# Sparse attention heads: mask and relative bias summed in device memory, loaded as one tile

## The chip, the cores and the metric

The kernel runs on one core of one Trainium2 chip. The metric is the device time in microseconds (us); a kernel is given by the median of its runs. One further execution is recorded by the hardware profiler, and all rows come from it. The engines are TensorE (PE; PEld is its weight load), VectorE (DVE), ScalarE (ACT), GpSimd (POOL) and SyncE (SP), which only issues transfers. SPq in a row is SP's instruction queue.

## What is computed

One encoder layer over 16 meta tokens and 1,024 tokens of width 1,024: a norm, one wide input projection, eight dense attention heads (branch A), eight sparse attention heads (branch B), gates, an output projection, and a mixture of experts. The change touches the scores of the sparse heads only:

```python
score = jnp.where(adm[None], score, NEG_INF)
_, idx = lax.top_k(score, k_sel)                      # 256 keys for each query
s = jnp.einsum('bqhd,bqkhd->bhqk', qb, ks) * scale_b
bias = rel_bias[t5_bucket(idx - pq[None, :, None])]   # by distance, one value a head
s = s.astype(jnp.float32) + jnp.transpose(bias, (0, 3, 1, 2)).astype(jnp.float32)
s = jnp.where(valid[:, None], s, NEG_INF)
p = jax.nn.softmax(s, axis=-1)
```

The kernel gathers nothing. It computes the scores of all keys and adds a mask of 0 or -1e30, so that the keys that were not selected vanish in the softmax.

## The kernel before

**Tiling.** Queries are cut into eight blocks of 128 rows. Block i may see the first WID[i] = 16 + 128 (i + 1) keys: 144, 272, 400, 528, 656, 784, 912 and 1,040. OFF holds the running sums of these widths; all eight side by side are OFF[8] = 4,736 columns. The mask is one tile of 128 x 4,736 in bf16 (`mask`). It depends on the query and the key, not on the head. The bias depends on the distance and the head, not on the block: `rel_d` in device memory holds for each head 128 copies of a row of 1,168 values, and `skewed[h]` reads it with a row pitch one shorter than the row, which gives the 128 x 1,040 table of block 7; block i uses the same table from column 128 (7 - i) on.

**Three stages matter.** (1) Projections, to about 548 us: PE runs `jobs`, ACT writes each result to one of four `stage` tiles, SP stores it (L391) and loads the next 1 MB weight piece (`piece_in`, L352); beside it DVE searches the top-k thresholds and writes `mask`. POOL forms the low-order parts of the weight pieces (L732). (2) Dense heads, 548 to about 701 us. (3) Sparse heads, to about 861 us. Stages 2 and 3 are one block of code with one pipeline: a table `turns`, built in Python, lists half heads s (s = 2 x head for blocks 0 to 3, s = 2 x head + 1 for blocks 4, 5, 7 and 6, `ORDER`), and in each half head one turn for each tile of 128 keys (5 or 9). `qk_after` says behind which turn a block's scores are computed ahead of use.

**Work of a block (`qk`, `row_max`, `exp`).** PE writes the scores of block g into PSUM. In a sparse head these are three passes of WID columns: identity times mask (L1144), query times leading part of the keys (L1147), query times rest of the keys (L1149). DVE adds the bias table `tb` to them, writes `sbias` and takes the row maximum in one instruction (L1284), and negates it (L1288). ACT takes the exponential into px, pxa or pxb, with the row's sum (L1233). In a dense head there is no bias; DVE only takes the maximum (L1291) and ACT reads PSUM.

**Work of a turn.** PE transposes up to four 128 x 128 tiles (L1191) into one of three PSUM banks; ACT copies the leading part (pH, L1245); DVE subtracts it (pL, L1310); three turns later PE multiplies both with the values (L1207, L1208). At a half head's end ACT copies the sum (oT, L1253), PE transposes it back (L1193), DVE adds two halves (otmp, L1317), POOL scales (otok, L1330).

**What sets the order.** Each engine runs its list in the written order. ACT's list has the copies pH and the exponentials in one row, and DVE's has pL and the row maxima in one row. PE opens a half head only when its four exponentials are done.

**POOL** prepares the next heads' inputs: at odd s the values (L1344 to L1349) and the next queries (L1355, L1357; L1361, L1363 for sparse heads), at even s the next keys (L1374, L1376), and `scaled` at each s. Its 16 half heads of the dense stage are s = 0 to 15. **SP** loads in the sparse stage, for each head in turn, QR (L1098), KR (L1103), tb (L1109) and VR (L1113, L1115), each behind the wait that frees its tile, all double buffered. With head 1 of the sparse ones it also loads the first branch weights (`wbr`, L1005).

## Time and profile before

| | |
|---|---|
| median of 3 runs | 1481.53 us (1480.89 to 1482.75) |
| the profiled execution | 1482.05 us |
| its span in the profile | 1480.3 us |
| PE, DVE, ACT, POOL busy | 93%, 70%, 45%, 28% of the span |
| dense heads | about 548 to 701 us |
| sparse heads | about 701 to 861 us |

The page of the profile gives the busy time of each engine, the span in 40 slices, the groups of instructions, and the transfers. Beside it, the trace can be asked for stretches (busy time of each engine in a window), for instructions in order of time, for waits, and for transfers. "[0.51 <-PE ps L1149]" at the end of a row means that the engine stood idle for 0.51 us before it and that PE's instruction of line 1149 ended this. A busy time holds the latency of each instruction, so that a pipelined engine can be busy without being at its peak.

### The profile page before, as it was taken

Reading aid. Unit: us, or ns where it says so; the run is one execution under the profiler, and the core shown is the slowest. Engines: PE = TensorE matmul, PEld = TensorE weight load, DVE = VectorE, ACT = ScalarE, POOL = GpSimd, SP = SyncE. Lnnn points to the kernel's source line nnn. Section 1 sums busy time; section 2 is a strip of 40 time slices with the busy share of each in tenths; the row PEclk is TensorE's granted clock in tenths of the full one; section 3 lists DMA queues with packets and bytes.
Section 4 is the critical chain, followed back from the end, with each engine's and each line's share of the span. In section 5 each row is a group of like instructions: output and inputs, shape, how many; then the busy total and the mean of one; then the engine's idle time right before and its main releaser. Section 6 shows DMA issues by size and latency. Waiting matters only on the chain. (4 is left out here: it accounts for less than half of the span.)

```text
span 1480.3 us, 21833 instructions
## 1 busy us (share of the span) xinstructions
PE 1383.0 (93%) x7358; PEld 1124.1 (76%) x7367; DVE 1029.0 (70%) x1959; ACT 665.5 (45%) x1179; POOL 416.9 (28%) x472
## 2 busy tenths in 40 slices
PE   5989999999999999999999979999959999999973
PEld 3779888888989758888788868899946777777741
DVE  4448999999980367777888863443287777777746
ACT  4347413322111146777777751022125666666622
POOL 1100335421112015545555303300021323323313
PEclk9999999999999999999999989999959999999996
DMA  6131321123232100303244044322178999999918
GB/s 210 30 124 57 126 77 50 48 88 104 73 97 93 51 0 2 80 1 108 55 98 102 23 147 147 110 100 82 48 292 345 364 355 348 364 376 369 349 54 329
DMA packets 89744, 217.42 MB, mean 147 GB/s; under 512 B 25825, under 2 KB 50945, under 8 KB 77369
## 3 DMA queue, kind: packets, MB, share of 16 engines
q1 hardware_dynamic: 79392, 194.65, 37.7%
q0 software_dynamic: 9216, 16.80, 3.0%
q10 hardware_dynamic: 1048, 4.82, 0.8%
q8 instruction: 53, 0.87, 0.3%
q14 instruction: 35, 0.28, 0.1%
HBM read 193.06 MB, written 44.73 MB: 161 GB/s over the span
## 5 line engine op out<-in xcount | busy, mean ns | idle before, releaser
L421 PE MATMUL ps<-hHi,g_lead 128*128 128x512 f32 (+2 forms) x480 | 184.8, 385 | 7.9 <-DVE g_rest L818 6.7
L315 DVE TENSOR_SCALAR_CACHE_REDUCE mask<-score,cand 128x272 bf16<-128x272 f32 (+6 forms) x224 | 185.5, 892 | 4.6 <-DVE cand L334 4.4
L2290 DVE TENSOR_TENSOR w_rest<-wgu,w_lead 128x1024 fp32r<-128x1024 f32 x128 | 156.2, 1223 | 46.6 <-ACT w_lead L2235 45.5
L422 PE MATMUL ps<-hLo,g_lead 128*128 128x512 f32 (+2 forms) x480 | 184.1, 384 | 0.0
L423 PE MATMUL ps<-hHi,g_rest 128*128 128x512 f32 (+2 forms) x480 | 183.0, 381 | 0.0
L1310 DVE TENSOR_TENSOR pL<-ps,pH 128x512 fp32r<-128x512 f32 (+3 forms) x224 | 124.6, 572 | 51.9 <-ACT pH L1245 49.3
L2235 ACT CAST w_lead<-wgu 128x1024 fp32r<-128x1024 f32 x124 | 130.8, 1055 | 48.6 <-PE ps L2178 48.6
L732 POOL TENSOR_TENSOR g_rest<-g_raw,g_lead 128x2048 fp32r<-128x2048 f32 x12 | 55.7, 4642 | 299.6 <-ACT g_lead L588 299.6
L1245 ACT CAST pH<-ps 128x512 fp32r<-128x512 f32 (+3 forms) x224 | 106.2, 493 | 59.3 <-PE ps L1191 59.1
L2176 PE MATMUL ps<-w_lead,x_lead 128*128 128x512 f32 x256 | 114.5, 447 | 4.0 <-DVE x_rest L2297 4.0
L2198 PE MATMUL ps<-wd,hmT 128*128 128x512 f32 x256 | 115.3, 593 | 1.6 <-DVE hmT L2313 1.0
L421 PEld LDWEIGHTS ps<-hHi,g_lead 128*128 128x128 f32 x480 | 91.0, 190 | 24.9 <-issue 7.0
L423 PEld LDWEIGHTS ps<-hHi,g_rest 128*128 128x128 f32 x480 | 91.2, 190 | 16.7
L422 PEld LDWEIGHTS ps<-hLo,g_lead 128*128 128x128 f32 x480 | 91.0, 189 | 15.0
L2178 PE MATMUL ps<-w_lead,x_rest 128*128 128x512 f32 x256 | 102.3, 400 | 0.0
L2177 PE MATMUL ps<-w_rest,x_lead 128*128 128x512 f32 x256 | 101.5, 396 | 0.0
L1207 PE MATMUL ps<-pH,VS 128*128 128x512 f32 (+3 forms) x224 | 94.6, 423 | 0.0
L2140 POOL DMA_INDIRECT ys_d<-ye,dk x32 | 32.3, 1010 | 216.0 <-DVE ye L2325 216.0
L2198 PEld LDWEIGHTS ps<-wd,hmT 128*128 128x128 f32 x256 | 46.2, 190 | 47.8 <-issue 47.8
L1208 PE MATMUL ps<-pL,VS 128*128 128x512 f32 (+3 forms) x224 | 79.1, 353 | 0.0
L619 ACT ACTIVATE stage<-ps 128x512 f32<-128x512 f32 x32 | 19.2, 599 | 112.0 <-PE ps L423 112.0
L2176 PEld LDWEIGHTS ps<-w_lead,x_lead 128*128 128x128 f32 x256 | 49.4, 193 | 21.0 <-issue 7.2
(363 smaller groups left out, 3421.1 us busy)
## 6 DMA issues: line engine op xcount, KB each, us to landing
wgu<-in_w_exp_gate SPq DMA_DIRECT2D x32, 1024.0 KB
wgu<-in_w_exp_up SPq DMA_DIRECT2D x32, 1024.0 KB
wd<-in_w_exp_down SPq DMA_DIRECT2D x32, 1024.0 KB, 12.0
g_raw<-in_w_in SPq DMA_DIRECT2D x16, 1024.0 KB, 5.6
gates_d<-stage SPq DMA_DIRECT2D x32, 256.0 KB, 2.0
gt<-gates_d SPq DMA_DIRECT2D x32, 256.0 KB, 3.2
rel_d<-rel_s ACTq DMA_DIRECT2D x1, 4672.0 KB
KR<-kb_d SPq DMA_DIRECT2D x16, 260.0 KB, 6.5
```

The source lines that it names most:

```text
L315: return dve.tensor_scalar(mask[:, OFF[i]:OFF[i + 1]], score[:, OFF[i]:OFF[i + 1]], thr, 0.0, op, ALU.add, accum_out=cnt[:, i:i + 1])
L421: pe.matmul(dst, x[0], y[0], start=(k == 0), stop=False)
L422: pe.matmul(dst, x[0], y[1], start=False, stop=False)
L423: return pe.matmul(dst, x[1], y[0], start=False, stop=(k == KT - 1))
L1245: act.copy(pH[n % RING][:, lo:512], bank_of(k)[:, lo:512]).then_inc(s_ld, 1)
L1310: dve.tensor_tensor(pL[n % RING][:, lo:512], bank_of(k)[:, lo:512], pH[n % RING][:, lo:512].bitcast(F32), ALU.subtract).then_inc(s_rs, 1)
L2176: pe.matmul(dst, xl[:, k, :], wl, start=(k == 0), stop=False)
L2177: pe.matmul(dst, xl[:, k, :], wr, start=False, stop=False)
L2178: mm = pe.matmul(dst, xr[:, k, :], wl, start=False, stop=(k == KT - 1))
L2198: mm = pe.matmul(ps[:, 5 + half, :], hmT[u % 2][:, k, :], wd[u][:, k, 512 * half:512 * (half + 1)], start=(k == 0), stop=(k == 1))
L2235: act.copy(w_lead[part][:, :, :, :], wgu[u][:, :, 2 * part:2 * part + 2, :]).then_inc(S["m_wl"], 1)
L2290: dve.tensor_tensor(w_rest[u][:, :, 2 * part:2 * part + 2, :], wgu[u][:, :, 2 * part:2 * part + 2, :], w_lead[part][:, :, :, :].bitcast(F3 ...
```

## The change

1. **Projections.** Beside jobs 4 to 35 SP issues two transfers each, 64 in all, from `rel_d` to a new array `bias_d` in device memory. It holds for each head the bias as 128 rows of 4,736 values in the mask's layout, 2.42 MB a head. The block's end waits for them.
2. **Dense heads.** POOL first writes `mask` to a new array `mask_d`, from bf16 to f32. Then, at the end of its half heads s = 3, 5, ... 17, it issues one accumulating transfer, `bias_d[h] += mask_d`, in device memory. Each waits for the one before (`s_jn`). As built it goes in 512 pieces of 1,184 values (4,736 bytes) each. `s_md` is waited for once, at s = 3.
3. **Sparse heads, loads.** In place of tb SP loads the sum into one tile `tbm`, 128 x 4,736 in f32, in four pieces a head, for blocks 0 and 1, 2 and 3, 4 and 5, and 6 and 7. There is one such tile; a piece is loaded when DVE has used the same piece for the head before (`s_mx`). The loads of queries, keys and values are spread between the pieces and keep their own waits. VR0 moves to where tb0 and VR0 lay.
4. **Sparse heads, compute.** The pass of L1144 is gone: two passes in place of three. DVE's instruction reads `tbm` instead of `tb`. It waits for the piece at every second block, not once a head.

```diff
@@ SP, projections
                     sp.dma_start(dst, src).then_inc(s_gds[n % 4], 16)
+                    if EARLY <= n < EARLY + 4 * H:
+                        if n == EARLY:
+                            sp.wait_ge(s_reld, 16)
+                        h, pair = divmod(n - EARLY, 4)
+                        for i in (2 * pair, 2 * pair + 1):
+                            c = P * (NB - 1 - i)
+                            sp.dma_start(bias_d[h, :, OFF[i]:OFF[i + 1]], skewed[h][:, c:c + WID[i]]
+                                         ).then_inc(s_bias, 16)
...
-                sp.wait_ge(s_reld, 16)
+                sp.wait_ge(s_bias, 16 * H * NB)
@@ SP, sparse heads (queries_in, keys_in and values_in hold the loads and waits of before)
+                def bias_in(h, pair):
+
+                    if h:
+                        sp.wait_ge(s_mx, 8 * (h - 1) + 2 * pair + 2)
+                    c = slice(OFF[2 * pair], OFF[2 * pair + 2])
+                    sp.dma_start(tbm[:, c], bias_d[h, :, c]).then_inc(s_tbs[pair], 16)
+
+                for h in range(2):
+                    queries_in(h)
+                    keys_in(h)
+                    values_in(h)
+                sp.wait_ge(s_hr, 2 * (H - 1))
+                for piece in range(2):
+                    load_branch_weights(sp, piece, s_wb)
+                for h in range(H):
+                    sp.wait_ge(s_jn, 16 * (h + 1))
+                    bias_in(h, 0)
+                    if 1 <= h < H - 1:
+                        values_in(h + 1)
+                    bias_in(h, 1)
+                    if h + 2 < H:
+                        queries_in(h + 2)
+                    bias_in(h, 2)
+                    if h + 2 < H:
+                        keys_in(h + 2)
+                    bias_in(h, 3)
@@ PE, qk of a sparse block
-                        for lo, hi in parts:
-                            pe.matmul(flat[:, o + lo:o + hi], identb[:, :], mask[:, OFF[i] + lo:OFF[i] + hi],
-                                      start=True, stop=False)
-                        for lo, hi in parts:
-                            pe.matmul(flat[:, o + lo:o + hi], q, kh[:, lo:hi], start=False, stop=False)
+                            pe.matmul(flat[:, o + lo:o + hi], q, kh[:, lo:hi], start=True, stop=False)
@@ DVE, row_max of a sparse block
                         if g % 8 == 0:
-                            dve.wait_ge(s_tb[h % 2], 16 * (h // 2 + 1))
                             dve.wait_ge(s_vr, 2 * H)
-                        c = P * (NB - 1 - i)
-                        dve.tensor_tensor_reduce(sbias[g % 2][:, 0:w], flat[:, o:o + w], tb[h % 2][:, c:c + w],
+                        if g % 2 == 0:
+                            dve.wait_ge(s_tbs[i // 2], 16 * (h + 1))
+                        dve.tensor_tensor_reduce(sbias[g % 2][:, 0:w], flat[:, o:o + w], tbm[:, OFF[i]:OFF[i + 1]],
@@ POOL, heads
+                def joined(h):
+
+                    if h:
+                        pool.wait_ge(s_jn, 16 * h)
+                    pool.dma_start(bias_d[h], mask_d[:, :], max_dma_last_dim=4736,
+                                   accum_op=ALU.add).then_inc(s_jn, 16)
+
+                pool.dma_start(mask_d[:, :], mask[:, :]).then_inc(s_md, 16)
...
                     if s >= 1:
                         scaled(s - 1)
+                    if s == 3:
+                        pool.wait_ge(s_md, 16)
+                    if s % 2 == 1 and 3 <= s < HH + 3:
+                        joined(s // 2 - 1)
```

The built programs show it at three places. PE, in the first sparse head, around the scores of block 6 (912 columns in two parts; con is the identity, QS the queries), before:

```order
L1191 MATMUL ps<-con,px_4845 128x128
L1144 MATMUL ps<-mask,identb 128x456 x2
L1147 MATMUL ps<-KH_138,QS_4872 128x456 x2
L1149 MATMUL ps<-KL_140,QS_4872 128x456 x2
L1207 MATMUL ps<-pH_4854,VS_4840 128x512
```

The same place now:

```order
L1221 MATMUL ps<-con,px_4910 128x128
L1177 MATMUL ps<-KH_138,QS_4937 128x456 x2
L1179 MATMUL ps<-KL_140,QS_4937 128x456 x2
L1237 MATMUL ps<-pH_4919,VS_4905 128x512
L1238 MATMUL ps<-pL_4923,VS_4905 128x512
```

The two instructions of the mask pass are gone, and nothing else moved. POOL, in the dense heads, from the queries of one head (q_lead, q_rest) to the keys (KH, KL) of the same head, before:

```order
L1355 CAST q_lead_135<-QTa 96x1024
L1357 TENSOR_TENSOR q_rest_137<-QTa,q_lead_135 96x1024
L1330 TENSOR_TENSOR otok_71<-otmp_4864,rec 128x4x64
L1374 CAST KH_139<-KTa 64x1040
L1376 TENSOR_TENSOR KL_141<-KTa,KH_139 64x1040
```

The same place now:

```order
L1385 CAST q_lead_135<-QTa 96x1024
L1387 TENSOR_TENSOR q_rest_137<-QTa,q_lead_135 96x1024
L1360 TENSOR_TENSOR otok_71<-otmp_4929,rec 128x4x64
L1413 DMA bias_d<-mask_d 512x1184
L1404 CAST KH_139<-KTa 64x1040
L1406 TENSOR_TENSOR KL_141<-KTa,KH_139 64x1040
```

The accumulating transfer, with its wait for the one before, stands ahead of the keys. SP, at the change from dense to sparse heads, before (the values of sparse head 1, the branch weights, then the loads of head 2):

```order
L1109 DMA tb_4877<-rel_d 128x1040
L1113 DMA VR_4879<-vb_d 128x8x64
L1115 DMA VR_4879<-vb_d 16x64
L1005 DMA wbr_4880<-in_w_branch_a 128x4x256
L1005 DMA wbr_4880<-in_w_branch_b 128x4x256
L1005 DMA wbr_4881<-in_w_branch_a 128x4x256
L1005 DMA wbr_4881<-in_w_branch_b 128x4x256
L1098 DMA QR_4870<-qb_d 64x1024 x2
L1103 DMA KR_4868<-kb_d 64x1040 x2
```

The same place now:

```order
L1123 DMA VR_4942<-vb_d 128x8x64
L1125 DMA VR_4942<-vb_d 16x64
L1019 DMA wbr_4944<-in_w_branch_a 128x4x256
L1019 DMA wbr_4944<-in_w_branch_b 128x4x256
L1019 DMA wbr_4945<-in_w_branch_a 128x4x256
L1019 DMA wbr_4945<-in_w_branch_b 128x4x256
L1132 DMA tbm<-bias_d 128x416
L1132 DMA tbm<-bias_d 128x928
L1109 DMA QR_4935<-qb_d 64x1024 x2
L1132 DMA tbm<-bias_d 128x1440
L1116 DMA KR_4933<-kb_d 64x1040 x2
L1132 DMA tbm<-bias_d 128x1952
```

The whole joined tile of the first sparse head is loaded here, behind the branch weights; before, its table had been loaded some 90 us earlier.

## Rows read from the trace of the kernel before

**Rows 1.** The page: busy us (share of the span) xinstructions of each engine.

```profile
PE 1383.0 (93%) x7358; PEld 1124.1 (76%) x7367; DVE 1029.0 (70%) x1959; ACT 665.5 (45%) x1179; POOL 416.9 (28%) x472
```

**Rows 2.** Stretches; columns: window, length, PE, PEld, DVE, ACT, POOL busy, PEclk, DMA share, GB/s.

```profile
200.00:240.00 40.00, 40.00 (x195) 35.46 (x194) 38.59 (x101) 11.48 (x33) 16.38 (x38) 1.00 0.14 47
572.00:610.00 38.00, 37.43 (x263) 31.91 (x262) 28.32 (x52) 27.49 (x65) 19.90 (x20) 1.00 0.33 78
720.00:740.00 20.00, 18.97 (x130) 15.96 (x130) 16.34 (x45) 14.61 (x36) 10.68 (x11) 1.00 0.41 97
740.00:760.00 20.00, 19.65 (x136) 16.69 (x136) 15.55 (x43) 14.66 (x34) 11.09 (x13) 1.00 0.45 111
```

**Rows 3.** PE in order of time around block 6: start us, us, instruction.

```profile
774.11 0.55 PE L1144 MATMUL ps<-mask,identb 128*128 128x456 bf16 x2
...
775.32 0.39 PE L1207 MATMUL ps<-pH,VS 128*128 128x512 f32 x1
```

**Rows 4.** PE, ACT and DVE in order of time, one sparse head.

```profile
758.64 0.66 PE L1191 MATMUL ps<-con,pxb 128*128 128x128 f32 x4
...
759.95 0.69 DVE L1310 TENSOR_TENSOR pL<-ps,pH 128x512 fp32r<-128x512 f32 x1 [0.81 <-ACT pH L1245]
...
761.09 0.42 ACT L1233 ACTIVATE px<-sbias,negm 128x144 f32<-128x144 f32 x1 [0.17 <-DVE negm L1288]
...
766.31 0.74 ACT L1233 ACTIVATE px<-sbias,negm 128x528 f32<-128x528 f32 x1 [0.33 <-DVE negm L1288]
...
769.78 0.84 ACT L1233 ACTIVATE pxb<-sbias,negm 128x656 f32<-128x656 f32 x1 [1.22 <-DVE negm L1288]
...
771.38 0.69 DVE L1310 TENSOR_TENSOR pL<-ps,pH 128x512 fp32r<-128x512 f32 x1
...
775.52 1.11 DVE L1284 CUSTOM_DVE_ANT_0 sbias<-ps,tb 128x912 f32<-128x912 f32 x1
...
776.86 1.06 ACT L1233 ACTIVATE pxb<-sbias,negm 128x912 f32<-128x912 f32 x1
...
778.06 0.66 PE L1191 MATMUL ps<-con,pxb 128*128 128x128 f32 x4 [0.76 <-ACT pxb L1233]
```

**Rows 5.** Waits from 701 to 862 us: who <- whom: us, times, longest.

```profile
PE ps L1191 <- ACT pxb L1233: 3.0, 4, 0.8
DVE sbias L1284 <- PE ps L1149: 2.1, 4, 0.5
```

**Rows 6.** POOL in order of time, two dense heads.

```profile
603.37 0.61 POOL L1330 TENSOR_TENSOR otok<-otmp,rec 128x256 f32<-128x256 f32 x1 [8.73 <-DVE otmp L1317]
...
622.82 0.61 POOL L1330 TENSOR_TENSOR otok<-otmp,rec 128x256 f32<-128x256 f32 x1 [8.74 <-DVE otmp L1317]
...
642.49 0.61 POOL L1330 TENSOR_TENSOR otok<-otmp,rec 128x256 f32<-128x256 f32 x1 [8.74 <-DVE otmp L1317]
```

**Rows 7.** Transfers from 90 to 130 us, by queue: packets, MB, share of 16 engines.

```profile
q10 hardware_dynamic: 1032, 4.78, 30.9%
```

**Rows 8.** One line of the code, POOL's gathers of 128 rows: duration ns min/median/max.

```profile
L2128 POOL DMA_INDIRECT xs<-xn_d,tk x28: 1017/1414/1419, 1102.2 to 1394.7; - x28
```

**Rows 9.** SP's loads in order of time, at the change to the sparse heads.

```profile
686.11 0.42 SPq L1005 DMA_DIRECT2D wbr<-in_w_branch_a x1
...
689.24 2.50 SPq L1098 DMA_DIRECT2D QR<-qb_d  x2
```

**Rows 10.** Stretches at the change to the sparse heads; columns as in Rows 2.

```profile
688.00:692.00 4.00, 4.00 (x29) 3.44 (x27) 3.30 (x7) 2.55 (x6) 3.68 (x4) 1.00 0.99 287
692.00:696.00 4.00, 4.00 (x29) 3.66 (x28) 3.01 (x7) 2.83 (x6) 0.42 (x1) 1.00 1.11 337
```

**Rows 11.** One line of the code, DVE's bias and maximum: duration ns min/median/max.

```profile
L1284 DVE CUSTOM_DVE_ANT_0 sbias<-ps,tb x64: 295/738/1232, 702.8 to 852.4; 128x144 f32<-128x144 f32 x8, 128x272 f32<-128x272 f32 x8, 128x400 f32<-128x400 f32 x8, 128x528 f32<-128x528 f32 x8
```

**Rows 12.** The page, costliest groups: busy, mean ns, idle before and its releaser.

```profile
L732 POOL TENSOR_TENSOR g_rest<-g_raw,g_lead 128x2048 fp32r<-128x2048 f32 x12 | 55.7, 4642 | 299.6 <-ACT g_lead L588 299.6
```

**Rows 13.** The page, transfers: KB each, us from issue to landing.

```profile
g_raw<-in_w_in SPq DMA_DIRECT2D x16, 1024.0 KB, 5.6
```

More of the change, by code:

```diff
@@ L128, in hybrid_layer @@
         rel_s = dram("rel_s", (H, REL), F32)
+        bias_d = dram("bias_d", (H, P, OFF[NB]), F32)
+        mask_d = dram("mask_d", (P, OFF[NB]), F32)
         qb_d = dram("qb_d", (4, P, T), F32)
@@ L305, in hybrid_layer @@
             sem, ["s_ij", "s_ie", "s_il", "s_wp", "s_wi", "s_lg", "s_re", "s_sc"])
-        s_gj, s_ge, s_tk, s_fl, s_uw = map(sem, ["s_gj", "s_ge", "s_tk", "s_fl", "s_uw"])
+        skewed = [bass.AP(tensor=rel_d.tensor, offset=h * P * REL + P - 1, ap=[[REL - 1, P], [1, L]])
+                  for h in range(H)]
+        s_gj, s_ge, s_tk, s_fl, s_uw, s_bias = map(sem, ["s_gj", "s_ge", "s_tk", "s_fl", "s_uw", "s_bias"])
         s_gds = [sem(f"s_gd{k}") for k in range(4)]
@@ L997, in hybrid_layer @@
         sbias = [at(f"sbias{k}", [P, L], F32, R_V + 4160 * k) for k in range(2)]
-        tb = [at(f"tb{k}", [P, L], F32, (R_Q + 8192, R_V + 8320)[k]) for k in range(2)]
-        VR = [at(f"VR{k}", [P, 9, HD], F32, (R_Q + 12352, R_V + 12480)[k]) for k in range(2)]
+        VR = [at(f"VR{k}", [P, 9, HD], F32, (R_Q + 8192, R_V + 12480)[k]) for k in range(2)]
+        tbm = at("tbm", [P, OFF[NB]], F32, R_Q + 12288)
+        assert 12288 + 4 * OFF[NB] <= 33280
         wbr = [at(f"wbr{k}", [P, 2, 4, 256], F32, R_K + 16640 + 8192 * k) for k in range(2)]
@@ L1006, in load_branch_weights @@
                              [:, :, 256 * piece:256 * (piece + 1)]).then_inc(done, 16)
-        s_qr, s_kr, s_vd, s_tb = ([sem(f"s_{nm}{k}") for k in range(2)] for nm in ("qr", "kr", "vd", "tb"))
+        s_qr, s_kr, s_vd = ([sem(f"s_{nm}{k}") for k in range(2)] for nm in ("qr", "kr", "vd"))
+        s_tbs = [sem(f"s_tb{pair}") for pair in range(4)]
+        s_md, s_jn = sem("s_md"), sem("s_jn")
         s_wb = sem("s_wb")
-        skewed = [bass.AP(tensor=rel_d.tensor, offset=h * P * REL + P - 1, ap=[[REL - 1, P], [1, L]])
-                  for h in range(H)]
         HH = 2 * H
@@ L1092, in _, with queries_in, keys_in, values_in @@
             def _(sp):
-                for h in range(H):
-                    j, u, k, hh = h // 2, h % 2, h % 2, H + h
-                    sp.wait_ge(s_hr, 6 if h < 2 else 2 * (hh - 2) - 1)
+                def queries_in(h):
+                    sp.wait_ge(s_hr, 6 if h < 2 else 2 * (H + h - 2) - 1)
                     for dup in range(2):
-                        sp.dma_start(QR[k][64 * dup:64 * (dup + 1), :], qb_d[j, 64 * u:64 * (u + 1), :]
-                                     ).then_inc(s_qr[k], 16)
+                        sp.dma_start(QR[h % 2][64 * dup:64 * (dup + 1), :],
+                                     qb_d[h // 2, 64 * (h % 2):64 * (h % 2 + 1), :]).then_inc(s_qr[h % 2], 16)
+                def keys_in(h):
                     if h >= 2:
-                        sp.wait_ge(s_hr, 2 * (hh - 2))
+                        sp.wait_ge(s_hr, 2 * (H + h - 2))
                     for dup in range(2):
-                        sp.dma_start(KR[k][64 * dup:64 * (dup + 1), :], kb_d[j, 64 * u:64 * (u + 1), :]
-                                     ).then_inc(s_kr[k], 16)
-                    if h == 1:
-                        sp.wait_ge(s_vr, 2 * H)
-                    if h >= 2:
-                        sp.wait_ge(s_mx, 8 * (h - 1))
-                    sp.dma_start(tb[k][:, :], skewed[h]).then_inc(s_tb[k], 16)
-                    if h >= 2:
-                        sp.wait_ge(s_vr, 2 * (hh - 1))
-                    c = slice(HD * h, HD * (h + 1))
+                        sp.dma_start(KR[h % 2][64 * dup:64 * (dup + 1), :],
+                                     kb_d[h // 2, 64 * (h % 2):64 * (h % 2 + 1), :]).then_inc(s_kr[h % 2], 16)
+                def values_in(h):
+                    k, c = h % 2, slice(HD * h, HD * (h + 1))
+                    if h:
+                        sp.wait_ge(s_vr, 2 * H if h == 1 else 2 * (H + h - 1))
                     sp.dma_start(VR[k][:, 0:8, :], vb_d[0:T, c].rearrange("(t p) c -> p t c", p=P)
@@ L1115, in _ @@
                     sp.dma_start(VR[k][0:META, 8, :], vb_d[T:L, c]).then_inc(s_vd[k], 16)
-                    if h == 1:
-                        sp.wait_ge(s_hr, 2 * (H - 1))
-                        for piece in range(2):
-                            load_branch_weights(sp, piece, s_wb)
+                def bias_in(h, pair):
[22 more added lines that the diff above has]
+                    bias_in(h, 3)
             @blk.tensor
```

1 line of the change is left out of this document (added).

## The prediction

> **What bounds the kernel now.** I read the page first. PE is busy 93% of the span [rows 1], and taken alone that would make every dropped PE pass a gain. The share is a mean over stages, so I went to the stretches of those that the change touches: the projections from 200 to 240 us, the dense heads, and the sparse heads. PE is busy 40.0 of 40, 37.4 of 38, and 19.0 to 19.65 of 20 us [rows 2]. The sparse heads seem as much bound by PE as the projections. But a busy PE there holds latencies and transposes, and a block of work has three engines in it. So I read one sparse head, 19.42 us long, in order of time [rows 4] and asked at each step who came last.
>
> It begins with PE's transposes at 758.64. ACT copies them, and DVE's pL at 759.95 has waited 0.81 us for ACT. Then DVE takes a row maximum, negates it, and ACT's exponential at 761.09 has waited 0.17 us for it. The next exponential at 766.31 waited 0.33 us for DVE, and that at 769.78 waited 1.22 us. From 771.38 DVE runs the maxima of blocks 5, 7 and 6 and the pL between them; the maximum of block 6 starts at 775.52 with no wait for PE. ACT's exponential at 776.86 follows it, and PE's transposes at 778.06 stood idle for 0.76 us for ACT before the next head began. What closes the loop is therefore ACT and DVE in turn, with PE in it once a head, for the first transposes. The reverse wait, DVE for PE's scores, is 2.1 us in all eight heads, four times, 0.5 at most; PE's wait for the last exponential of a head is 3.0 us [rows 5].
>
> **The mask pass.** Around block 6 the three passes take from 774.11 to 775.32, 1.21 us [rows 3]: 0.40 us a pass for 912 columns, 0.44 ns a column. A head has 4,736 columns, so 2.1 us a head, and for eight heads 16.8 us. That is the most that it can bring, if PE were the bound.
>
> What it brings in the loop above is less. The scores' end decides only where DVE waits for it: 2.1 us in all [rows 5]. Where ACT waits for PE's transposes, the passes ahead of these make them later, but DVE is then still at its own list (block 5 to 7: it goes from 771.38 to the last maximum with pL and maxima alone), so what ACT gains it waits for at DVE. Since scores come earlier, a part of the 2.1 us stays in the loop at ACT and DVE. I take 1.0 us, between 0 and 2.1. PE's idle time grows by nearly the 16.8 us instead.
>
> DVE's instruction reads another tile of the same shape and type, with nothing else changed: 0. Its wait at each second block finds the piece loaded long before, except in the first head (below). Behind the wait stand pL and the maxima of the same list. I take 0, at most 1 us over 32 waits.
>
> **The projections.** SP issues 64 transfers more among those of the weight pieces. They read and write 19.4 MB each way over some 30 jobs. PE is at 40.0 of 40 us in this stage, with the transfer engines at a share of 0.14 and 47 GB/s [rows 2]. A weight piece lands 5.6 us after its issue [rows 13]; POOL, which works on it, idles 299.6 us in 12 waits for ACT in this stage [rows 12], so a piece may land some us later without anyone noticing. Cover: PE's own matmuls, and the pieces' buffers. I take 0. Without the cover a piece late by its own 5.6 us would cost PE that much once or twice; I keep up to 3 us for it in the range.
>
> **The accumulating transfers.** Eight of them, issued by POOL, about one per head of the dense stage. The trace shows no such transfer, so I bound its time T. The nearest packets in size are those of the broadcast to `rel_d`: 1,032 packets took 30.9% of 16 engines' time in 40 us [rows 7], 197.8 engine-us, 0.192 us for each 4.6 KB. The new transfer has 512 pieces of 4.7 KB, 32 per engine. One pass is 6.1 us, if reading both operands costs no more than a copy; two passes are 12.3 us, if each operand is one; three are 18.4 us, if the sum is written in a pass of its own. To these comes POOL's own work for the pieces: its gathers of 128 rows hold it 1.4 us [rows 8], so 512 pieces are between 1.4 and 5.6 us. T lies between 7.5 and 24.0 us; I take the middle, near two passes and 3.5 us, 15.8.
>
> The rows say what T would have to be to hurt. POOL waits before each transfer for the one before. POOL's `otok` of one place in the dense head comes at 603.37, 622.82 and 642.49 [rows 6], so the transfers are issued 19.45 to 19.67 us apart, and below that T costs nothing. Above it POOL is late by T - 19.5 at each of seven waits. It idles 8.7 us a head before that place [rows 6]; since the lateness adds up, this slack is used once: the cost is 7 x (T - 19.5) - 8.7 us. It is nothing to T = 20.7, +3 us at 21.2, +12.3 at 22.5 and +22.8 at 24.0. At my value it is 0. Behind POOL's wait stand the keys of the next head (KH, KL) and the scaling, and behind the keys PE's scores.
>
> The Trainium skill, page "Collectives: The Full Stack", section "The bandwidth ceiling: the fold count and why AG ≠ RS ≠ AR", says that an add in the transfer engines costs no time for the adding, but needs two source reads and so goes at half a copy's rate. By it T is at most 12.3 + 5.6 = 17.9 us, as an estimate, against at most 11.7 us at a copy's price; either is under a head's length, and the third pass, with which alone the change could turn slower, would not exist. No row here shows an adding transfer, so I keep the third pass in the bounds.
>
> The cast of the mask into device memory is one more transfer of POOL at the start, with the first values following behind it on POOL. It is of the size of one pass, and runs beside PE's first dense scores: 0, since it only holds POOL for the issue, 1.4 to 5.6 us against the 8.7 us that POOL idles per head [rows 6].
>
> **The first loads of the sparse heads.** SP issues the branch weights from 686.11 and the loads of the next head from 689.24 [rows 9]. From 688 to 696 us the transfer engines are full, a share of 0.99 to 1.11, at 287 to 337 GB/s [rows 10]. The change puts the first head's sum there, 2.4 MB, where 0.5 MB of the next table lay: 1.9 MB more, at 337 GB/s 5.6 us more of full engines, and beside it one accumulating transfer, issued in the same microseconds. DVE needs the first piece (blocks 0 and 1, 0.2 MB) at 702.8 [rows 11]; that is 13 us behind the issue. The later pieces are needed some us after that. Bounds: 0, and +5 us if the whole of the extra traffic ends in front of DVE. I take +0.5, since the first piece stands ahead of the queries and is small. At later heads a piece is loaded nearly a head ahead, with the share at 0.41 to 0.45 [rows 2]: 0.
>
> The Trainium skill, page "DMA: Bandwidth & Descriptors", section "Issuing engines are not separate DMA queues", says that transfers of all issuing engines run on the same 16 and interleave. By that rule the pieces from SP and the accumulating transfer from POOL share the full stretch, which speaks for a cost here. The trace agrees that the stretch has no room, but shows no accumulating transfer.
>
> **The sum.** Mask pass -1.0, waits and projections 0, accumulating transfers 0, first loads +0.5: -0.5 us. On the profiled execution of 1482.05 us that is 1481.5. This execution stands 0.5 us above the median of the runs shown, 1481.53, so I forecast 1481.0 us: no change that can be told, since 0.2% (about 3 us) is what a measurement of this kernel can tell from none.
>
> **Rivals.**
>
> *PE is the bound after all.* For it: 19.65 us busy in 20 [rows 2], and PE's single wait of a head, 0.76 us [rows 4], is short; with the passes gone ACT's and DVE's waits for PE shrink too. Against it: at the head's end PE waits for ACT, and ACT's exponentials wait 0.3 to 1.2 us for DVE. Fully, 1481.5 - 16.8 = 1464.7 us; by half, about 1473. Chance 0.15.
>
> *An accumulating transfer outlasts a dense head.* This is the case on the slower side. Place: POOL's wait for the transfer before, at the end of each second half head from 610 us on, ahead of the next keys. Price: 7 x (T - 19.5) - 8.7 us. It decides from T = 20.7 us. With T = 22.5, 1481.5 + 12.3 = 1493.8 us; at the upper bound of T, about 1504. For it: three passes and a slow issue are within the bounds, and in the dense heads these transfers share the engines with others, at a share of 0.33 [rows 2]. Against it: it needs nearly the upper ends of both terms. Chance 0.21.
>
> *The first loads come late.* DVE stands at its first maxima for the pieces: up to +5 us, 1486. Chance 0.06.
>
> *It doesn't do what it says* would be that the pass is dropped but comes back as time elsewhere on PE; the order shows only the two instructions gone, so I give it no chance of its own.
>
> **How the numbers follow.** Forecast 0.58, PE-bound 0.15, accumulating 0.21, late loads 0.06. The forecast's own range is 1478.5 to 1484.5: the mask pass 0 to -2.1, up to 3 us for projections and the extra waits. The range reaches below to the half gain, 1474 with a little of it spared, and above to 1492, where the accumulating rival is at T = 22.2. Left out are the full gain (0.08) and the larger part of the accumulating rival (0.11). Faster by over 0.2%: the PE-bound rival and 0.02 of the forecast, 0.17. Slower: the accumulating rival less 0.01 where T is just at the limit, and the late loads: 0.26. Within: 0.57.
>
> **What the profile after would show.** Right: in the sparse heads PE's busy time falls from 19.0 to 19.65 to about 17 of 20 us, while the distance between the first transposes of two heads stays at 19.0 to 19.4 us; PE's waits for ACT and DVE grow by some 15 us over the stage; DVE's waits for PE's scores vanish. POOL's wait for a transfer in the dense heads stays within its idle time, with the landing of the accumulating transfer at 8 to 19 us and the heads at 19.5 to 19.7 us. The sparse heads begin at about 701 us, with a wait of DVE for a piece below 1 us. Wrong: the head's length falls by up to 2.1 us (then PE was the bound, and the loop that I read was not tight); POOL waits for transfers over 8.7 us and PE for the keys (then T was too low); PE waits in the projections for weight pieces (then the 64 transfers weren't hidden).

## The result and the profile after

| | before | changed |
|---|---|---|
| median | 1481.63 us (4 runs) | 1494.75 us (4 runs, 1492.86 to 1496.42) |
| ratio | | 1.0085, 95% interval 1.0073 to 1.0097 |
| the profiled execution, its span | 1482.05, 1480.3 us | 1492.86, 1491.1 us |
| DVE's first L1284 / L1314 to its last | 702.8 to 852.4 us | 708.0 to 864.6 us |

The change costs 13 us, 0.85%. The forecast was 1481.0 us with a range to 1492.0, so the prediction is wrong. The page's engine line, beside [rows 1]:

```profile
PE 1371.6 (92%) x7254; PEld 1113.6 (75%) x7255; DVE 1021.2 (68%) x1959; ACT 664.5 (45%) x1179; POOL 426.6 (29%) x481
```

PE is busy 11.4 us less and the kernel is slower. (Dropping the pass alone takes 16.8 us off PE's busy time, in experiment 8; behind the waits below the matmuls take longer.) The stretches, with the columns of [rows 2]; the last one is a sparse head that nothing disturbs:

```profile
600.00:660.00 60.00, 59.08 (x413) 50.44 (x413) 45.95 (x82) 43.61 (x105) 33.98 (x33) 1.00 0.81 167
660.00:700.00 40.00, 39.26 (x274) 33.23 (x273) 30.17 (x55) 28.69 (x68) 22.67 (x22) 1.00 0.79 180
700.00:720.00 20.00, 14.17 (x82) 12.33 (x82) 9.68 (x32) 8.37 (x21) 11.26 (x11) 0.83 1.04 261
720.00:740.00 20.00, 16.99 (x110) 13.64 (x108) 15.36 (x41) 14.35 (x35) 11.32 (x11) 1.00 1.05 284
740.00:760.00 20.00, 13.90 (x88) 11.79 (x89) 13.29 (x37) 11.31 (x26) 7.23 (x9) 0.95 1.04 261
800.00:820.00 20.00, 17.42 (x117) 14.79 (x118) 15.98 (x44) 14.22 (x33) 11.35 (x11) 1.00 0.70 205
```

The dense heads go on at their pace. From 700 to 760 us the transfer engines are full (share 1.04 to 1.05, against 0.41 to 0.45 in [rows 2]), and PE, DVE and ACT have all lost busy time. DVE in order of time names what it waits for, at blocks 0 of head 0 and 2 of heads 1 and 2:

```profile
708.00 0.31 DVE L1314 CUSTOM_DVE_ANT_0 sbias<-ps,tbm 128x144 f32<-128x144 f32 x1 [6.16 <-DMA tbm<-bias_d]
...
731.87 0.57 DVE L1314 CUSTOM_DVE_ANT_0 sbias<-ps,tbm 128x400 f32<-128x400 f32 x1 [1.34 <-DMA tbm<-bias_d]
...
756.34 0.57 DVE L1314 CUSTOM_DVE_ANT_0 sbias<-ps,tbm 128x400 f32<-128x400 f32 x1 [5.11 <-DMA tbm<-bias_d]
```

These are 12.6 us in three waits, and there is no further one. The waits of the kernel before [rows 5] have none of this kind. The stretch from DVE's first L1314 to its last is 156.6 us, where L1284 took 149.6 before; with the first wait of 6.16 us, which lies ahead of it, 162.8. That is 13.2 us more, where the pass should have given something back.

Why the first piece is late: SP's list at the change to the sparse heads, and how long the three pieces issued from 685 to 693 us took to land (min/median/max):

```profile
684.69 0.42 SPq L1019 DMA_DIRECT2D wbr<-in_w_branch_a  x1
...
687.31 2.95 SPq L1132 DMA_DIRECT2D tbm<-bias_d  x2
...
735.09 7.64 SPq L1132 DMA_DIRECT2D tbm<-bias_d  x1
742.77 4.13 SPq L1109 DMA_DIRECT2D QR<-qb_d  x2
746.95 1.86 SPq L1132 DMA_DIRECT2D tbm<-bias_d  x1
```

```profile
DMA to landing us min/median/max: 19.2/20.5/21.6
```

The first piece is issued at 687.3 us, behind 2 MB of branch weights, and 0.2 MB takes about 20 us. An accumulating transfer is issued at 687.9 us. In the later rows SP itself is held: at 735.09, as soon as DVE is through with blocks 2 and 3 of head 1, the piece for these blocks of head 2 is issued; the issue alone lasts 7.64 us, the piece lands 21.1 us behind its start, and DVE still waits for it until 756.3. The queries and the next piece stand behind it on SP.

The accumulating transfers in the quiet dense heads and the one of 687.9 us, issue to landing; and the share of the engines that their queue (q0, GpSimd's) took from 560 to 702 us:

```profile
DMA to landing us min/median/max: 15.1/15.1/16.5
```

```profile
DMA to landing us min/median/max: 21.3/21.3/21.3
```

```profile
q0 software_dynamic: 2995, 13.81, 50.3%
```

50.3% of 142 us, times 16, over 2,995 packets is 0.381 us a packet, twice the 0.192 of the broadcast's [rows 7], and 512 of them are 12.2 us of all 16 engines. In this kernel POOL never waits for one; between two of them it idles for DVE, as before:

```profile
590.10 1.18 POOL L1413 DMA_DIRECT2D bias_d<-mask_d  x1
...
602.39 0.61 POOL L1360 TENSOR_TENSOR otok<-otmp,rec 128x256 f32<-128x256 f32 x1 [7.55 <-DVE otmp L1347]
...
609.54 1.04 POOL L1413 DMA_DIRECT2D bias_d<-mask_d  x1
```

### The profile page after: what moved, and what is told of

The parts are those of the page before. It is cut to its first block and busy times, and to the rows that moved or that the text cites. A ratio compares the mean times of both kernels' runs of the same rounds, so it can differ in the third digit from the quotient of the medians.

```text
span 1491.1 us, 21721 instructions
## 1 busy us (share of the span) xinstructions
PE 1371.6 (92%) x7254; PEld 1113.6 (75%) x7255; DVE 1021.2 (68%) x1959; ACT 664.5 (45%) x1179; POOL 426.6 (29%) x481
## 5 line engine op out<-in xcount | busy, mean ns | idle before, releaser
L632 ACT ACTIVATE stage<-ps 128x512 f32<-128x512 f32 x32 | 19.2, 599 | 112.1 <-PE ps L436 112.0
L1360 POOL TENSOR_TENSOR otok<-otmp,rec 128x256 f32<-128x256 f32 x32 | 19.6, 613 | 159.3 <-DVE otmp L1347 159.3
## 6 DMA issues: line engine op xcount, KB each, us to landing
wd<-in_w_exp_down SPq DMA_DIRECT2D x32, 1024.0 KB, 12.4
```

## The experiments

Ratios are against the kernel before on the same chip. *Theory A*: three of the eight accumulating transfers, 12 us of full engines each, fall into the stretch in which the sparse heads load, and with those loads they are more than the engines can move. *Theory B*: the loads alone are too much, since the bias of a head is 2.42 MB in place of 0.53.

**1. Without the accumulating transfers**

```diff
-                    if s % 2 == 1 and 3 <= s < HH + 3:
-                        joined(s // 2 - 1)
...
@@ SP
-                    sp.wait_ge(s_jn, 16 * (h + 1))
```

> The changed kernel without its eight accumulating transfers, and without SP's waits for them; the mask is left out of the result, the loads of the bias tile and the 64 transfers of the projections stay. Theory A (the last three accumulating transfers, 12 engine-us each, fill the engines in which the first three sparse heads load): DVE's waits for pieces fall from 12.6 us to 0 to 2, the time to 1481 to 1484. Theory B (the loads alone are too much: branch weights, doubled bias bytes, small packets): waits stay at 8 us or more, 1490 to 1495.

Measured: 1480.28 us, ratio 0.9988 (0.9978 to 0.9997), and no wait of DVE for a piece. Pieces issued from 685 to 693 us land in:

```profile
DMA to landing us min/median/max: 8.1/9.3/12.7
```

8 to 13 us in place of 19 to 22, though the first of them goes out at 690.0 us and not at 687.3. Theory B falls: branch weights, large pieces and all 64 transfers of the projections are still there. What the engines had to move from 684 to 765 us, by queue, before, here, and in the changed kernel:

```profile
q1 hardware_dynamic: 8203, 9.38, 45.4%
```

```profile
q1 hardware_dynamic: 11145, 17.56, 74.2%
```

```profile
q1 hardware_dynamic: 9309, 14.31, 56.8%
q0 software_dynamic: 1584, 7.27, 45.3%
```

By the first two, the bias as a 2.42 MB tile adds 28.8% of 81 us, 23 us of full engines, in four heads; this fits. Three accumulating transfers are 37 us more: 74.2% + 45.3% is 119.5%, some 16 us more than the stretch holds. The changed kernel's loads got only 56.8% in that time.

**2. The same transfers, earlier**

```diff
-        s_md, s_jn = sem("s_md"), sem("s_jn")
+        s_md, s_jn = sem("s_md"), [sem(f"s_jn{h}") for h in range(H)]
...
-                    if h:
-                        pool.wait_ge(s_jn, 16 * h)
...
-                    if s % 2 == 1 and 3 <= s < HH + 3:
-                        joined(s // 2 - 1)
+                    if 1 <= s <= H:
+                        joined(s - 1)
```

> The changed kernel with the accumulating transfers issued at each half head from the first on, with no wait between them (a semaphore for each), so that they are done by about 680 us if 12 to 13 us of full engines is their price. Theory A: the stretch from 686 to 760 us loses three of them; DVE's waits 0 to 3 us, 1481 to 1484. Theory B: as without them, waits of 8 us or more, 1490. A new cost would show as POOL held by the issue, or PE waiting for keys, in the dense heads.

Measured: 1479.14 us, ratio 0.9984 (0.9974 to 0.9994). All eight sums are made, none of them issued behind 644 us, and DVE waits for no piece. Landing of the pieces issued from 685 to 693 us, and DVE's L1314 from first to last:

```profile
DMA to landing us min/median/max: 9.1/9.8/12.4
```

```profile
L1314 DVE CUSTOM_DVE_ANT_0 sbias<-ps,tbm x64: 297/739/1231, 703.5 to 852.3; 128x144 f32<-128x144 f32 x8, 128x272 f32<-128x272 f32 x8, 128x400 f32<-128x400 f32 x8, 128x528 f32<-128x528 f32 x8
```

148.8 us, 0.8 less than before [rows 11]. The dense heads with the transfer engines full for 60 us, and two stretches of the sparse heads:

```profile
600.00:660.00 60.00, 59.12 (x412) 50.38 (x411) 45.01 (x80) 43.89 (x103) 35.41 (x35) 1.00 1.06 228
700.00:720.00 20.00, 17.52 (x118) 14.80 (x116) 16.28 (x48) 14.35 (x34) 10.28 (x10) 1.00 0.71 206
740.00:760.00 20.00, 17.65 (x121) 15.38 (x122) 15.75 (x44) 14.33 (x36) 11.07 (x12) 1.00 0.70 207
```

PE is busy 59.12 of 60 us with the transfer engines at 1.06. So the same work costs nothing that can be seen in the dense heads and 13 us at their end: the place decides. This kernel is some 15 us below the changed one, and its interval against the kernel before lies wholly below 1. The loads issued beside the transfers are slow here too (one of the values took 36.2 us to land), but no engine waited for them.

**3. Two of the eight in place of three.** Each one head earlier, with its wait:

```diff
-                    if s == 3:
+                    if s == 1:
...
-                    if s % 2 == 1 and 3 <= s < HH + 3:
-                        joined(s // 2 - 1)
+                    if s % 2 == 1 and s < HH + 1:
+                        joined(s // 2)
```

> The changed kernel with each accumulating transfer issued one head earlier (at half heads 1, 3, ... 15), with its waits. Two of eight, about 24 us of full engines, then fall behind 686 us in place of three, and the last one is issued at about 714 us. Theory A (the sum of what the engines have to move behind 686 us decides): 12 us of backlog go, DVE's waits fall from 12.6 us to 0 to 5, 1480 to 1486. Theory B (the burst at 686 to 692 decides, with the accumulating transfer of 688 us in it): about as the changed kernel, 8 us of waits or more, since that transfer is still there: 1489 to 1494.

Measured: 1488.34 us, ratio 1.0041 (1.0027 to 1.0056). DVE's waits:

```profile
708.72 0.31 DVE L1314 CUSTOM_DVE_ANT_0 sbias<-ps,tbm 128x144 f32<-128x144 f32 x1 [4.87 <-DMA tbm<-bias_d]
...
733.27 0.57 DVE L1314 CUSTOM_DVE_ANT_0 sbias<-ps,tbm 128x400 f32<-128x400 f32 x1 [2.96 <-DMA tbm<-bias_d]
```

7.8 us in place of 12.6, in heads 0 and 1. Neither expectation is met; B's lower ends (8 us, 1489) miss by little, A's upper ones (5 us, 1486) by more. The first wait, 4.87 us, is nearly that of the changed kernel, since at 689.9 us an accumulating transfer is still issued into the burst; the one in head 2 is gone with the transfer that fell there (that in head 1 is 2.96 in place of 1.34). I read this as two places with a price each, the burst at 686 us and the backlog behind it; how a single profile divides the waits among the heads is loose (experiment 7), so the sum of 7.8 is the firmer number.

**4. The burst without the weights.** The 2 MB of branch weights loaded ahead of head 6's pieces:

```diff
-                for piece in range(2):
-                    load_branch_weights(sp, piece, s_wb)
                 for h in range(H):
+                    if h == 6:
+                        for piece in range(2):
+                            load_branch_weights(sp, piece, s_wb)
```

> The changed kernel with the 2 MB of branch weights loaded before the pieces of sparse head 6, not before those of head 0. Theory A: the first wait of DVE, 6.2 us, shrinks to 0 to 3 since 2 MB (5 to 6 us of full engines) go, the waits in heads 1 and 2 (1.3 and 5.1 us) shrink as well, since the backlog starts lower: 1484 to 1489. Theory B: all waits go, 1481 to 1484. If the weights don't matter: 1494.

Measured: 1482.22 us, ratio 0.9999 (0.999 to 1.0009), with all three accumulating transfers within some 3 us of where they were (688.9, 711.2 and 731.8 us). Pieces issued from 685 to 693 us, and all of DVE's waits for pieces (us, times):

```profile
DMA to landing us min/median/max: 4.3/6.3/8.1
```

```profile
  DMA tbm<-bias_d: 1.2, 1
```

The first piece is issued at 685.8 us, 3.1 us ahead of the accumulating transfer (0.5 in the changed kernel), and lands in time; DVE then frees its part of the tile in time for the next head's. In numbers this is Theory B's forecast and a miss of Theory A's. Theory B stays out by experiments 1 and 2, where the loads and the weights are all there and nobody waits. What fails is Theory A as a rule of bytes alone: 6 us of traffic taken from in front of the first piece remove 11.4 us of waits, where 12 us taken from behind it (experiment 3) removed 4.8.

**5. The first head's pieces earlier.** First, the four pieces moved ahead of the weights and their wait (and dropped for head 0 in the loop behind, which the cut leaves out):

```diff
+                sp.wait_ge(s_jn, 16)
+                for pair in range(4):
+                    bias_in(0, pair)
                 sp.wait_ge(s_hr, 2 * (H - 1))
                 for piece in range(2):
                     load_branch_weights(sp, piece, s_wb)
```

> The changed kernel with the four pieces of sparse head 0 loaded as soon as their sum is there (about 605 us), in the dense heads. Theory A: 2.4 MB leave the full stretch, the first wait of 6.2 us goes; heads 1 and 2 lose at least half of their 6.4 us: 1481 to 1487. Rival (only the order of the queue counts, and the backlog of accumulating transfers stays): the first wait goes, the other two stay, 1488 to 1490.

Measured: 1497.15 us, ratio 1.0107 (1.009 to 1.0124). It missed: I had not read what stands ahead of that place in SP's list, the wait for the tile of head 1's values. SP's rows:

```profile
685.23 3.35 SPq L1132 DMA_DIRECT2D tbm<-bias_d  x4
...
691.72 12.97 SPq L1019 DMA_DIRECT2D wbr<-in_w_branch_b  x1
```

The pieces went out at 685.2 us, not at 605. Head 0 waited for none, but the weights and all behind them came later: the last weights' issue held SP for 12.97 us, and heads 1 and 2 waited 16.1 us in three waits. The edit as it was meant puts the pieces ahead of those values, behind `sp.wait_ge(s_hr, 2 * (H - 1) - 1)`, since the tile shares its place with the dense queries:

> The changed kernel with the four pieces of sparse head 0 ahead of the values of sparse head 1 in SP's list, behind the wait for the last dense queries, so that they are issued at about 667 us. In the kernel with the pieces merely ahead of the weights they stood behind the wait for those values and were issued at 685.2, as late as in the changed kernel. 2.4 MB leave the full stretch. If only the bytes ahead of the pieces count: no wait in head 0, less than 4 us in heads 1 and 2, 1481 to 1486. If the accumulating transfers alone decide: heads 1 and 2 still wait 6 us or more, 1487 to 1490.

Measured: 1482.71 us, ratio 1.0008 (0.9999 to 1.0018); waits for pieces:

```profile
  DMA tbm<-bias_d: 2.1, 1
```

The pieces went out at 668.2 us. Head 0 and head 1 wait for none, head 2 for 2.1 us: the first expectation is met. Three accumulating transfers are still issued behind 686 us, so they alone don't make the 12.6 us either.

**6. Small pieces.** Heads 1 to 7 load 32 columns a piece and use head 0's bias and mask in all other columns:

```diff
-                    c = slice(OFF[2 * pair], OFF[2 * pair + 2])
+                    c = slice(OFF[2 * pair], OFF[2 * pair] + 32 if h else OFF[2 * pair + 2])
```

> The changed kernel where the pieces of sparse heads 1 to 7 are 32 columns wide (128 bytes a row; the rest of the bias tile keeps head 0's values, so bias and mask of head 0 are used in all heads), head 0's pieces whole. The accumulating transfers and all else stay. Theory A (neither the sums nor the bias bytes alone, but both together): head 0 waits as before, about 6 us, heads 1 and 2 don't: 1486 to 1489. If the sums alone were too much for the loads of queries, keys and values: waits of 5 us or more in heads 1 and 2, or POOL late with the keys.

Measured: 1488.61 us, ratio 1.005 (1.0034 to 1.0067).

```profile
709.08 0.31 DVE L1314 CUSTOM_DVE_ANT_0 sbias<-ps,tbm 128x144 f32<-128x144 f32 x1 [5.22 <-DMA tbm<-bias_d]
...
732.67 0.57 DVE L1314 CUSTOM_DVE_ANT_0 sbias<-ps,tbm 128x400 f32<-128x400 f32 x1 [2.08 <-DMA tbm<-bias_d]
```

Head 0 waits as expected (5.22 us), head 2 no more; that head 1 still waits 2.08 us was not expected; its pieces stand in SP's queue behind head 0's large ones, but that this is the cause was not tried. So the bytes of the later heads' pieces have a part of about 5 of the 12.6 us, and none without the accumulating transfers (experiment 1).

**7. Early transfers with the first pieces ahead of the weights, and the changed kernel again**

> The changed kernel with the accumulating transfers at half heads 1 to 8, a semaphore for each, and head 0's pieces at about 667 us. With the accumulating transfers moved alone DVE waited for no piece, so the second edit should find nothing to gain: within 1 us of that kernel, 1478 to 1481. More than 2 us below it would mean that the burst at 686 us costs something that no wait shows.

Measured: 1479.48 us, ratio 0.9985 (0.9976 to 0.9995); no wait for a piece. The kernel as built is not the one that this expectation describes. It takes the first edit of experiment 5 and not the second: head 0's pieces stand ahead of the weights but behind the values of head 1, and SP issues them at 686.6 us, not at 667:

```profile
686.58 1.84 SPq L1132 DMA_DIRECT2D tbm<-bias_d  x4
```

So it shows this much: with the accumulating transfers early, the order that cost 16.1 us of waits in experiment 5 costs nothing, and pieces ahead of the weights gain nothing over experiment 2 (1479.14 us). Pieces at 667 us together with early accumulating transfers were not tried.

> The changed kernel again, for a profile and a ratio beside the others on one chip: 1492 to 1497, DVE waiting for pieces of heads 0 to 2 by 10 us or more. If the waits lie in other heads or their sum moves by over 5 us, single profiles of this collision can't be compared to a few us.

Measured: 1496.11 us, ratio 1.0089 (1.0072 to 1.0106).

```profile
709.78 0.31 DVE L1314 CUSTOM_DVE_ANT_0 sbias<-ps,tbm 128x144 f32<-128x144 f32 x1 [5.96 <-DMA tbm<-bias_d]
...
758.76 0.57 DVE L1314 CUSTOM_DVE_ANT_0 sbias<-ps,tbm 128x400 f32<-128x400 f32 x1 [6.15 <-DMA tbm<-bias_d]
```

12.1 us, near the 12.6, but in two waits: the 1.34 us of head 1 is gone and head 2's is longer. In these two profiles the sum of the waits is steady, their division isn't.

**8. What the mask pass is worth.** In the kernel before, the pass alone dropped (the lines of L1144 in the diff above):

> The kernel before with the mask pass alone dropped (the mask is left out of the result; tables, loads and everything else as before). If the sparse heads are closed by ACT and DVE: heads of 19.43 and 18.78 us in turn as in the changed kernel's last heads, 0.8 to 1 us less in all, 1480.5. If PE is the bound: 2.1 us a head, 1465.

Measured: 1479.29 us, ratio 0.9984 (0.9974 to 0.9993). DVE's bias and maximum, first and last start, and a stretch as in [rows 2]:

```profile
L1281 DVE CUSTOM_DVE_ANT_0 sbias<-ps,tb x64: 298/740/1231, 702.4 to 851.1; 128x144 f32<-128x144 f32 x8, 128x272 f32<-128x272 f32 x8, 128x400 f32<-128x400 f32 x8, 128x528 f32<-128x528 f32 x8
```

```profile
740.00:760.00 20.00, 17.78 (x125) 15.51 (x124) 16.31 (x44) 14.80 (x35) 11.12 (x13) 1.00 0.49 119
```

148.7 us from first to last against 149.6 [rows 11]: the pass gives 0.9 us in the sparse heads. (It is 148.7 or 148.8 too in the kernels of experiments 1, 2 and 7 without the pass and without a wait.) PE's busy time falls from 19.65 to 17.78 of 20 us and nobody uses it. The medians differ by 2.2 us; what the further 1.3 us are I can't say. Then the loop that I had read was loosened, by halving the width of DVE's bias and maximum, with the pass kept and without it:

```diff
+                        w = w // 2 if g >= 8 * H + 8 else w
                         dve.tensor_tensor_reduce(sbias[g % 2][:, 0:w], flat[:, o:o + w], tb[h % 2][:, c:c + w],
```

> The kernel before, where from sparse head 1 on DVE's bias and maximum covers only the first half of a block's columns (the second half of the scores is left out of the bias and the maximum, ACT still takes the exponential of the full width). That takes about 1.06 ns a column x 2,368 = 2.5 us of DVE a head, 17.6 us for seven heads. If DVE is in the loop: 5 to 10 us less (PE, busy 95 to 98%, ends it then): 1472 to 1477. If PE is the bound already: 1480 to 1482.

> The kernel before with both edits: half the width of DVE's bias and maximum from sparse head 1 on, and no mask pass (both parts are left out of the result). If the loop of ACT and DVE hid the pass, the pass is worth more here than its 1 us in the kernel without the DVE edit: 4 us or more below the kernel with the DVE edit alone, 1465 to 1471. If the pass is hidden for another reason (PE's weight loads, ACT alone): within 2 us of it.

Measured: 1475.42 us, ratio 0.9955 (0.9938 to 0.9972), with the pass, and 1471.12 us, ratio 0.9925 (0.9908 to 0.9942), without it. The same DVE line in each, and, with the pass, DVE's waits for PE's scores (us, times), which were 2.1, 4 [rows 5]:

```profile
L1285 DVE CUSTOM_DVE_ANT_0 sbias<-ps,tb x64: 222/490/1231, 702.4 to 847.3; 128x72 f32<-128x72 f32 x7, 128x136 f32<-128x136 f32 x7, 128x200 f32<-128x200 f32 x7, 128x264 f32<-128x264 f32 x7
```

```profile
  PE ps L1149: 9.7, 19
```

```profile
L1282 DVE CUSTOM_DVE_ANT_0 sbias<-ps,tb x64: 223/489/1231, 703.9 to 843.3; 128x72 f32<-128x72 f32 x7, 128x136 f32<-128x136 f32 x7, 128x200 f32<-128x200 f32 x7, 128x264 f32<-128x264 f32 x7
```

With half the width alone the time is as expected. Without the pass as well it is 4.3 us lower, also as expected, if just above the range, and DVE's waits for PE's scores are back at 2.0 us in three waits. From first to last it is 144.9 and 139.4 us, but these two profiles enter the sparse heads 1.5 us apart, so the six whole heads between DVE's first maximum of head 1 and that of head 7 are the cleaner measure. These two instructions in the kernel before, without the pass, with half the width, and with both edits:

```profile
722.16 0.29 DVE L1284 CUSTOM_DVE_ANT_0 sbias<-ps,tb 128x144 f32<-128x144 f32 x1
...
837.41 0.30 DVE L1284 CUSTOM_DVE_ANT_0 sbias<-ps,tb 128x144 f32<-128x144 f32 x1
```

```profile
721.61 0.30 DVE L1281 CUSTOM_DVE_ANT_0 sbias<-ps,tb 128x144 f32<-128x144 f32 x1
...
836.22 0.30 DVE L1281 CUSTOM_DVE_ANT_0 sbias<-ps,tb 128x144 f32<-128x144 f32 x1
```

```profile
721.75 0.22 DVE L1285 CUSTOM_DVE_ANT_0 sbias<-ps,tb 128x72 f32<-128x72 f32 x1
...
832.82 0.22 DVE L1285 CUSTOM_DVE_ANT_0 sbias<-ps,tb 128x72 f32<-128x72 f32 x1
```

```profile
723.15 0.22 DVE L1282 CUSTOM_DVE_ANT_0 sbias<-ps,tb 128x72 f32<-128x72 f32 x1
...
829.86 0.22 DVE L1282 CUSTOM_DVE_ANT_0 sbias<-ps,tb 128x72 f32<-128x72 f32 x1
```

The six heads last:

| | with the pass | without | the pass is worth |
|---|---|---|---|
| DVE at full width | 115.25 us | 114.61 us | 0.64 us |
| DVE at half width | 111.07 us | 106.71 us | 4.36 us |

The medians say the same more loosely, 2.2 and 4.3 us, with intervals that overlap. There is one profile of each kernel, but heads of undisturbed kernels repeat to some 0.02 us. That shows both: ACT and DVE close the loop at full width, and PE is close behind them.

## Why the prediction was wrong, point by point

- **What bounds the sparse heads: right.** The pass was put at 1.0 us and is 0.9, though PE was busy 95 to 98% there. Loosening DVE's part moves the time; dropping PE's alone hardly does. The ceiling of 2.1 us a head if PE were the bound is reached by PE's busy time (16.8 us less in experiment 8), but by no kernel's duration: at half of DVE's width the pass is worth 0.7 us a head. The signs that were named for this came in the undisturbed heads, with PE busy 17.42 of 20 us and heads of 19.4 and 18.8 us in turn.
- **The accumulating transfer's time: right in the dense heads, too low beside the loads.** T was taken at 15.8 us and is 15.1 us in the dense heads: two passes' worth of packets (12.2 us) and 3 us around them, of which POOL is held for 1.04. The Trainium skill, page "Collectives: The Full Stack", section "The bandwidth ceiling: the fold count and why AG ≠ RS ≠ AR", says of the reducing step of a ring that its add needs two source reads and so goes at half a copy's rate; the trace agrees for this transfer, with 0.381 against 0.192 us a packet. The one of 687.9 us took 21.3 us, above the 20.7 from which the prediction lets T cost time. POOL doesn't wait for it in the changed kernel, only because DVE's stall had already made the next one late (it is issued 26.4 us behind). Where that stall is gone POOL does wait: 6.9 us in experiment 4 and 11.5 us in the second kernel of experiment 5. In neither did PE wait for POOL's keys. That the changed kernel's 1494.75 us lies near the 1493.8 that the prediction gave for this rival is chance: its mechanism isn't what the trace shows.
- **Projections and the cast of the mask: right, as far as can be told.** PE's waits in the projections are the same ones, the longest group 7.3 us in place of 6.7. DVE would have begun its first L1314 at 701.84 us, against 702.8 before; but this start lies anywhere from 701.8 to 703.9 in all kernels here, with the 64 transfers and without, so neither a cost nor a gain of 1 us could be seen.
- **The first loads: the step that failed.** It was put at +0.5 us, with +5 as its bound, and DVE waited 6.16 us for head 0's first piece. The term counted 1.9 MB more of pieces against the engines' rate, 5.6 us, and named "one accumulating transfer, issued in the same microseconds", but gave it no price, though the step before had worked out 12.3 us of full engines for it. With it the sum in front of the first piece would have been, as an estimate, 6 us of weights (2 MB at 337 GB/s) and 12 us shared with the accumulating transfer and the piece: some 19 us behind 686, later than DVE's 702.8. The piece landed at 707.8. Experiments 1 and 2 take away the accumulating transfer, experiment 4 the weights, and the wait goes each time. "The first loads come late" was among the rivals, with a chance of 0.06 and at most 5 us: the right place at much too small a price. The Trainium skill, page "DMA: Bandwidth & Descriptors", section "Issuing engines are not separate DMA queues", says that transfers of SP and GpSimd run on the same engines and interleave; the trace agrees, with 20.5 us for the first piece beside GpSimd's transfer, and 8.1 and 9.8 in experiments 1 and 2 without it. By this rule the forecast should have priced the collision, not named it.
- **"At later heads: 0": failed too.** The share of 0.41 to 0.45 was read as room. Two further accumulating transfers fall behind 700 us (714.2 and 735.1), some 24 us of full engines, and there is one tile, so that a late DVE frees the next head's pieces late. Heads 1 and 2 waited 6.45 us. That makes 12.6 us of waits where the forecast had 0.5.
- **A cost that I had not seen at all.** While PE waited its granted clock began to fall, and it stayed low for some us behind the wait. Stretches of the changed kernel, columns as in [rows 2], and one of PE's instructions in the second:

```profile
700.00:708.00 8.00, 2.70 (x24) 2.46 (x23) 0.79 (x4) 1.67 (x3) 6.20 (x7) 0.94 1.04 277
708.00:716.00 8.00, 7.63 (x34) 6.57 (x34) 6.28 (x18) 4.50 (x12) 2.32 (x3) 0.64 1.04 281
```

```profile
709.20 0.63 PE L1237 MATMUL ps<-pH,VS 128*128 128x512 f32 x1
```

  PE is busy 2.70 of 8 us (not at all from 704 to 708), then has a granted clock of 0.64 in the mean, so the lower of its two levels (1.2 and 2.4 GHz) for most of that stretch; 512 columns take 0.63 us there and 0.39 in [rows 3]. From DVE's first maximum to that of head 1 it is 20.9 us (to 728.9), with no wait for a piece between, and 19.2 in the kernel with the transfers earlier: 1.7 us on top of the wait of 6.2. A pair of other waits fits. In experiment 4 the wait of 1.24 us in head 2 left the clock at 1.00, and heads 2 and 3 were 1.3 us longer than in experiment 2. In the second kernel of experiment 5 the wait of 2.07 us at the same place was followed by clocks of 0.50 and 0.77, and the same heads were 4.1 us longer. No experiment changed the clock alone, so that it makes the whole of these 1.7 us isn't shown.

The sum by the trace: 12.6 of waits, 1.7 behind the first wait, less 0.9 for the pass and 1.0 by which this profile reached the sparse heads earlier is 12.4 us; the last L1314 starts 12.2 us later than before. Behind it the changed profile is 1.4 us shorter, so that the two profiled executions differ by 10.8 us, and the medians by 13.1. The profiled execution is the fastest of the four; where the 2.3 us between them lie is open.

## What to carry to other kernels

A transfer has two prices: how long its issuer waits for it, and how long it keeps all the engines busy for the others. Sum the second over every stretch that it touches, with the transfers that are already there, and put it against the length of the stretch; here a mean share of 0.45 had no room for three times 12 us and bias loads of 2.42 MB a head. And place background transfers by when the loads of others are due, not by when their own result is: here it decides between +13 and -2 us.

## What I had not expected of the hardware

- An accumulating transfer from device memory to device memory (512 pieces of 4,736 bytes) takes 12.2 us of all 16 engines, 0.381 us a packet where the broadcast's took 0.192, and 15.1 us from issue to landing in the quiet dense heads.
- The issue itself can hold SP: 7.64 us for one piece of the bias, 12.97 us for one of the weights (experiment 5), and 9.17 us for 4 KB of values at 752.8 us, so it isn't the size of what is issued. A piece's issue takes 0.33 us at the median, and from 684 to 760 us no single issue in experiments 1 and 2, which have no accumulating transfer there, takes over 2.5. What stands behind a held issue on SP is late by that much, whatever it is.
- Eight of them run nearly back to back beside the dense heads, from 572 to 677 us (share 1.06 from 600 to 660 us), and PE is busy 59.12 of 60 us there, against 59.06 before.
